# Output projection of a transformer block: four weight panels in buffers of their own, an earlier first load, the norm's running sums in PSUM

## The reference

```
y = (g_a * y_a + g_b * y_b) @ w_mix_out
x = layer_norm(ALPHA * x + mod(1, 2) * y, ln2_g, ln2_b)
h = x * (1.0 + mod(2, 1)) + mod(2, 0)
x = layer_norm(ALPHA * x + 0.5 * mod(2, 2) * swiglu(h, ffn2_w_in, ffn2_w_out), ln3_g, ln3_b)
```

## Time and profile before

| | |
|---|---|
| median of 3 runs | 1108.89 us (1108.68 to 1109.15) |
| the profiled execution | 1108.3 us, its span 1106.1 us |
| TensorE busy | 1096.5 us, 99% of the span |
| DVE / POOL / ACT busy | 527.5 / 521.6 / 412.9 us |
| granted clock | 0.999 in the mean |

### The profile page before, as it was taken

The page is one execution under the profiler, slowest core; times in us unless marked ns, Lnnn a source line. Parts: engine busy times, 40 slices in busy tenths (PEclk is TensorE's granted clock), DMA queues, the critical chain, the costliest instruction groups (busy, mean ns, idle before and its releaser), DMA issues.

```text
span 1106.1 us, 15348 instructions
## 1 busy us (share of the span) xinstructions
PE 1096.5 (99%) x5574; PEld 895.8 (81%) x5574; DVE 527.5 (48%) x924; ACT 412.9 (37%) x665; POOL 521.6 (47%) x277
## 2 busy tenths in 40 slices
PE   9999999999999999999999999999999999999997
PEld 6788888888888997875578887898888888888887
DVE  6677756441121269268747678784322223111105
ACT  4453232223222274278623233357322222232223
POOL 1044544444444464459824453646444444445452
PEclk9999999999999999999999999999999999999999
DMA  9555554322333272210145653323433332233322
GB/s 373 200 195 203 184 174 173 106 95 86 95 98 105 74 258 96 87 38 20 49 132 201 219 182 132 120 72 134 146 121 114 114 114 95 90 92 101 105 69 76
DMA packets 53460, 142.11 MB, mean 128 GB/s; under 512 B 5793, under 2 KB 13985, under 8 KB 52129
## 3 DMA queue, kind: packets, MB, share of 16 engines
q1 hardware_dynamic: 52400, 136.25, 36.8%
q10 hardware_dynamic: 1008, 5.17, 1.3%
HBM read 139.31 MB, written 2.10 MB: 128 GB/s over the span
## 4 chain that ended last, share of the span: by engine, by line
PE 95%; DVE 2%; DMA 1%; ACT 1%; issue 1%; SPq 0%; POOL 0%; ACTq 0%; DVEq 0%
PE psum L667 29%; PE psum L669 29%; PE psum L668 29%; PE psum L1055 2%; PE psum L1106 2%; PE psum L1134 2%; DMA ada_first<-in_ada 1%; PE psum L990 1%; PE psum L697 1%; DVE acc L1919 0%; PE psum L1120 0%; DVE blocked L1663 0%; PE psum L1026 0%; POOL w_lo L568 0%; PE psum L796 0%
## 5 line engine op out<-in xcount | busy, mean ns | idle before, releaser
L568 POOL TENSOR_TENSOR w_lo<-raw,w_hi 128x1024 fp32r<-128x1024 f32 x177 | 437.1, 2473 | 532.8 <-ACT w_hi L1230 532.5
L667 PE MATMUL psum<-h_hi,w_hi 128*128 128x512 f32 (+1 forms) x1008 | 381.7, 379 | 1.1 <-POOL h_lo L617 1.0
L668 PE MATMUL psum<-h_lo,w_hi 128*128 128x512 f32 (+1 forms) x1008 | 378.7, 376 | 0.0
L669 PE MATMUL psum<-h_hi,w_lo 128*128 128x512 f32 (+1 forms) x1008 | 378.6, 376 | 0.0
L1230 ACT ACTIVATE w_hi<-raw 128x1024 fp32r<-128x1024 f32 x183 | 191.7, 1052 | 153.1 <-PE psum L669 95.8
L667 PEld LDWEIGHTS psum<-h_hi,w_hi 128*128 128x128 f32 x1008 | 189.6, 188 | 41.0 <-issue 4.5
L669 PEld LDWEIGHTS psum<-h_hi,w_lo 128*128 128x128 f32 x1008 | 189.7, 188 | 34.4
L668 PEld LDWEIGHTS psum<-h_lo,w_hi 128*128 128x128 f32 x1008 | 189.7, 188 | 33.8
L1919 DVE SCALAR_TENSOR_TENSOR acc<-ada_raw,cact,acc 128x512 f32<-128x512 f32 x98 | 138.2, 1446 | 15.6 <-DMA ada_raw<-in_ada_w 15.5
L667 PE MATMUL psum<-act_hi,w_hi 128*128 128x512 f32 (+1 forms) x396 | 145.3, 367 | 0.0
L669 PE MATMUL psum<-act_hi,w_lo 128*128 128x512 f32 (+1 forms) x396 | 144.7, 365 | 0.0
(11 more groups left out here) (269 smaller groups left out, 1009.0 us busy)
## 6 DMA issues: line engine op xcount, KB each, us to landing
raw<-in_ffn_in SPq DMA_DIRECT2D x82, 512.0 KB, 3.3
ada_raw<-in_ada_w SPq DMA_DIRECT2D x112, 256.0 KB, 3.5
raw<-in_ffn_out SPq DMA_DIRECT2D x32, 448.0 KB, 3.3
raw<-in_mix_w SPq DMA_DIRECT2D x27, 512.0 KB, 3.3
ada_first<-in_ada SPq DMA_DIRECT2D x8, 1024.0 KB, 11.1
raw<-in_ffn_out SPq DMA_DIRECT2D x16, 512.0 KB, 3.5
raw<-in_branch_w SPq DMA_DIRECT2D x8, 512.0 KB, 3.8
raw<-in_mixout_w SPq DMA_DIRECT2D x8, 512.0 KB, 3.3
```

What stands on the lines that cost most here:

```text
L568: gp.tensor_tensor(w_lo[:, slot, :], raw[:, slot % 2, :], w_hi[:, slot, :].bitcast(F32), ALU.subtract).then_inc(split_done, 1)
L667: pe.matmul(o_, w_hi[:, wslot, ws], xh, start=first, stop=False)
L668: pe.matmul(o_, w_hi[:, wslot, ws], xl, start=False, stop=False)
L669: return pe.matmul(o_, w_lo[:, wslot, ws], xh, start=False, stop=last)
```

## The change

- **Own buffers.** Panels 4 to 7 of the output projection are split into `late_hi` and `late_lo`, which lie where the branches' operands lay; they wait for the branches to be through, and for no slot. The feed-forward's first four panels then wait for the panel that used their slot, eight before.
- **Order of splits on ACT.** A list, MIXOUT_SPLIT, says how many panels are split ahead of the square of tile m; panel 11 is split between the first two late squares, ahead of the first root. POOL splits the feed-forward's first four panels ahead of all low parts of h.
- **First load.** SP issues panel 0 of the projection ahead of the last six modulation pieces.
- **Fold.** The third fold stands on DVE behind mixed_lo(7), and `sum_modulation` on TensorE in panel 1, behind its third k.
- **PSUM.** The running sum lies in bank 3, the squares of tiles 1 to 4 alternate in banks 5 and 4; the last sum goes back to `scr`.

```diff
@@
 LOW_BANK = {1: 4, 2: 0}
+OWN = 4
+OWN_FROM = B_MIXOUT + KT - OWN
+SUMS_BANK, SQ_BANK = 3, 4
+MIXOUT_SPLIT = [4, 6, 8, 9, 11]
@@
         o_lo = at("o_lo", [P, 4, T], R + 81920, F32R)
         w1k = at("w1k", [P, PAIRS, 256], R + 73728)
         tokens = at("tokens", [P, TT, D], O_HHI)
+        late_hi = at("late_hi", [P, OWN, 1024], R + 57344, F32R)
+        late_lo = at("late_lo", [P, OWN, 1024], R + 73728, F32R)
         mixed_hi = at("mixed_hi", [P, KT, T], R, F32R)
         mixed_lo = at("mixed_lo", [P, KT, T], R + 16384, F32R)
         tab = at("tab", [P, 2, 2, T], R + 32768)
@@
             for i in range(3 * KT):
                 if i >= 3:
                     branch_panel(i + 2)
+                if i == 3 * KT - 3:
+                    panel(B_MIXOUT, mixout_w[0, :, :], slot=B_MIXOUT % 2)
                 for q in range(2 * (i % 3), 2 * (i % 3) + 2):
                     ada_unit("mix", i // 3, q)
-            for m in range(KT):
+            for m in range(1, KT):
                 p = B_MIXOUT + m
                 panel(p, mixout_w[m, :, :], slot=p % 2)
             feed_forward(2)
@@
                 gp.wait_ge(split_hi, p + 1)
                 gp.tensor_tensor(w_lo[:, slot, :], raw[:, slot % 2, :], w_hi[:, slot, :].bitcast(F32),
+                                 ALU.subtract).then_inc(split_done, 1)
+            def own_split(i):
+                p = OWN_FROM + i
+                gp.wait_ge(split_hi, p + 1)
+                gp.tensor_tensor(late_lo[:, i, :], raw[:, p % 2, :], late_hi[:, i, :].bitcast(F32),
                                  ALU.subtract).then_inc(split_done, 1)
             def splits(start, end):
@@
                             alibi((u + 3) // 2, ((u + 1) % 2,))
                         elif u < 7:
                             split(B_BRANCH + u - 3, (B_BRANCH + u - 3) % 4)
-                    splits(B_BRANCH + 4, end + 3)
+                    splits(B_BRANCH + 4, OWN_FROM)
+                    for i in range(OWN):
+                        own_split(i)
+                    splits(B_FFN2, B_FFN2 + GROUP)
                 for m in (1, 2, 3, 4):
                     low(L, 0, m)
-                split(end + 3, 3)
+                if L == 1:
+                    split(end + 3, 3)
                 for m in (6, 7):
                     low(L, 0, m)
                 for m in LOW_POOL[1]:
@@
         @block.tensor
         def _(pe):
-            def product(o_, wslot, kk, xh, xl, first, last):
+            def product(o_, wslot, kk, xh, xl, first, last, w=(w_hi, w_lo)):
                 ws = slice(kk * P, (kk + 1) * P)
-                pe.matmul(o_, w_hi[:, wslot, ws], xh, start=first, stop=False)
-                pe.matmul(o_, w_hi[:, wslot, ws], xl, start=False, stop=False)
-                return pe.matmul(o_, w_lo[:, wslot, ws], xh, start=False, stop=last)
+                pe.matmul(o_, w[0][:, wslot, ws], xh, start=first, stop=False)
+                pe.matmul(o_, w[0][:, wslot, ws], xl, start=False, stop=False)
+                return pe.matmul(o_, w[1][:, wslot, ws], xh, start=False, stop=last)
             def panel_over_h(p, wslot, b, h_wait=None):
@@
                 for k in range(4):
                     ins = product(bank(b + 3), p % 4, 4 + k, o_hi[:, k, :], o_lo[:, k, :], k == 0, k == 3)
                 ins.then_inc(panels_used, 1)
+            def mixout_panel(m):
+                p = B_MIXOUT + m
+                return (p - OWN_FROM, (late_hi, late_lo)) if p >= OWN_FROM else (p % 4, (w_hi, w_lo))
             pe.wait_ge(br_mixed, KT - 1)
-            sum_modulation(2, 3, 6)
             for m in range(LATE[2][0]):
+                slot, w = mixout_panel(m)
                 p = B_MIXOUT + m
                 if m >= 2:
                     pe.wait_ge(z_done, Z0[2] + m - 1)
@@
                 for k in range(KT):
                     if m == 0:
                         pe.wait_ge(br_split, k + 1)
-                    ins = product(bank(m % 2), p % 4, k, mixed_hi[:, k, :], mixed_lo[:, k, :],
-                                  k == 0, k == KT - 1)
+                    ins = product(bank(m % 2), slot, k, mixed_hi[:, k, :], mixed_lo[:, k, :],
+                                  k == 0, k == KT - 1, w)
+                    if m == 1 and k == 2:
+                        sum_modulation(2, 3, 6)
                 ins.then_inc(panels_used, 1)
             pe.wait_ge(ada_taken, 2)
             for h in range(2):
                 for i, m in enumerate(LATE[2]):
                     p = B_MIXOUT + m
+                    slot, w = mixout_panel(m)
                     if h == 0 and i < 2:
                         pe.wait_ge(z_done, Z0[2] + m - 1)
                     else:
@@
                     if h == 0:
                         pe.wait_ge(split_done, p + 1)
                     for k in range(KT):
-                        ins = product(psum[:, (m + h) % 2, part(h)], p % 4, k, mixed_hi[:, k, part(h)],
-                                      mixed_lo[:, k, part(h)], k == 0, k == KT - 1)
+                        ins = product(psum[:, (m + h) % 2, part(h)], slot, k, mixed_hi[:, k, part(h)],
+                                      mixed_lo[:, k, part(h)], k == 0, k == KT - 1, w)
                         if k == KT - 1:
                             ins.then_inc(panels_used if h else half_made, 1)
                         if h == 1:
@@
             def split(p, slot, filled):
                 act.wait_ge(raw_landed[slot % 2], 16 * filled)
-                need(act, panels_used, p - 3)
+                if isinstance(p, int) and OWN_FROM <= p < B_FFN2:
+                    act.wait_ge(panels_used, B_MIXOUT)
+                    act.activation(late_hi[:, p - OWN_FROM, :], raw[:, slot % 2, :], ACT.Copy).then_inc(split_hi, 1)
+                    return
+                if isinstance(p, int) and B_FFN2 <= p < B_FFN2 + OWN:
+                    act.wait_ge(panels_used, p - 3 - OWN)
+                else:
+                    need(act, panels_used, p - 3)
                 if isinstance(p, int) and p == P_GATE:
                     act.activation(gate_w[:, :].rearrange("p (k c) -> p k c", c=32),
                                    raw[:, slot % 2, :].rearrange("p (k c) -> p k c", c=P)[:, :, 0:32],
@@
                 act.wait_ge(z_done, Z0[L] + m + 1)
                 if m >= 2:
                     act.wait_ge(q_added, QA0[L] + max(m - 2, 1))
-                act.activation(scr[:, 2 + m % 2, :], X[:, m, :], ACT.Square).then_inc(sq_done, 1)
+                to = scr[:, 2 + m % 2, :]
+                if L == 2:
+                    to = bank(SQ_BANK + m % 2) if m else scr[:, 1, :]
+                act.activation(to, X[:, m, :], ACT.Square).then_inc(sq_done, 1)
             def first_row(k):
@@
                 for i in range(late):
                     square_half(L, i, 0)
+                    if L == 2 and i == 0:
+                        split_before(p0 + 1)
+                if L == 1:
+                    split_before(p0 - 2)
                 root(0)
                 if L == 2:
                     square_half(2, 0, 1)
@@
                 act.activation(mixed_hi[:, m, :], tab[:, m % 2, 0, :], ACT.Copy).then_inc(br_hi, 1)
             act.preload_act_table(ACT.Sqrt)
             for m in range(LATE[2][0]):
-                split_before(B_MIXOUT + m + 1)
+                split_before(B_MIXOUT + MIXOUT_SPLIT[m] - 3)
                 square(2, m)
-            split_before(B_FFN2 - 2)
             norm_halves(2)
             feed_forward(2)
             act.preload_act_table(ACT.Sqrt)
@@
                     dve.wait_ge(s_added, summed[0])
                 summed[0] += 1
                 dve.wait_ge(z_done, Z0[L] + m + 1)
-                a = X[:, 0, :] if m == 1 else scr[:, 0, :]
-                dve.tensor_tensor(scr[:, 0, :], a, X[:, m, :], ALU.add).then_inc(s_added, 1)
+                total = bank(SUMS_BANK) if L == 2 else scr[:, 0, :]
+                a = X[:, 0, :] if m == 1 else total
+                to = scr[:, 0, :] if m == LATE[L][0] - 1 else total
+                dve.tensor_tensor(to, a, X[:, m, :], ALU.add).then_inc(s_added, 1)
             def squares(L, m):
                 dve.wait_ge(sq_done, Q0[L] + m + 1)
                 if m > 1:
                     dve.wait_ge(q_added, QA0[L] + m - 1)
+                if L == 2:
+                    dve.tensor_tensor(scr[:, 1, :], bank(SQ_BANK + m % 2), scr[:, 1, :], ALU.add).then_inc(q_added, 1)
+                    return
                 a = scr[:, 2, :] if m == 1 else scr[:, 1, :]
                 dve.tensor_tensor(scr[:, 1, :], a, scr[:, 2 + m % 2, :], ALU.add).then_inc(q_added, 1)
@@
                 dve.wait_ge(x_scaled, 8 * (L - 1) + m + 1)
                 dve.wait_ge(s_added, summed[0])
                 summed[0] += 1
-                dve.tensor_tensor(scr[:, 0, :], scr[:, 0, :], X[:, m, :], ALU.add).then_inc(s_added, 1)
+                total = bank(SUMS_BANK) if L == 2 else scr[:, 0, :]
```

(5 more changed lines are left out.)

## The result

The changed kernel takes **1113.1 us** in the median of 7 runs (1112.37 to 1113.93), the kernel before, run beside it, 1108.75 us (1108.46 to 1109.15). The ratio is 1.0040, with a 95% interval from 1.0030 to 1.0049: slower, by 4.4 us. The forecast was 1109.4, with a range up to 1111.4. It was wrong: the change is slower, where I had forecast no difference that can be measured. The profiled execution took 1113.6 us, its span is 1111.4 (before 1108.3 and 1106.1), so the traces have 5.3 us to explain.

A forecast was written before the change was run, and what follows sets the result against it. TensorE, busy 1096.5 of 1106.1 us, was taken to bound the kernel. +1.35 (the new gap, with the fold's -1.14 inside) - 0.84 = +0.5 us on the median 1108.89 gave 1109.4 us, range 1106.8 to 1111.4.

The forecast's parts named there:

- Part 1: Moving the third fold and its product into panel 1: the 1.58 us gap goes, the 0.44 product stays, -1.14 us.
- The two readiness margins: In the fold's move: mixed_lo(7) ready 1.1 us before TensorE needs it, the fold 1.2 us before its product.
- Part 2: Panel 0 of the output projection loaded before six modulation loads: nothing lost, by some 2 us; needed for Part 1.
- Part 3: Own buffers, earlier splits: ACT's panel 10 split delays tile 4's square; new 2.5 us TensorE gap before third late half.
- the round: Cycle of the raw double buffer: load 3.3, ACT to POOL 1.13, POOL 2.38, issue 0.04, together 6.85 us.
- Rival 2: The new gap drops TensorE's clock to 1.2 GHz for 24 products: +2.9, in all +3.4, 1112.3 us; chance 0.10.
- Part 4: No weight splits behind the first root: DVE's held sum of squares falls from 1.26 to 0.42 us, -0.84 us.
- Sums and squares in PSUM: no cost, no gain by themselves: On DVE: at most 0.05 us more each, hidden; the 2 us blocks they end had not delayed TensorE.
- the factor column: DVE's 8-column, SBUF-only operation before tile 0's square: held by a POOL split; without a hold the sum would be -0.1.
- rival 1: No new gap before the third late half, panel 10's split coming in time: -2.0 us, 1106.9; chance 0.22.

The follow-up runs named there:

- fold_back: fix_order with the third fold and its product ahead of the output projection again; 1107.22 us, ratio to the kernel before 0.9988.
- load_back: fix_order with panel 0 of the projection loaded behind the six modulation pieces again; 1108.46 us, ratio to the kernel before 0.9998.
- fix_order: The changed kernel with ACT splitting panel 10 between the second and third late squares, panel 11 behind the third; 1106.17 us, ratio to before 0.9979.
- one_number: The changed kernel with MIXOUT_SPLIT's last entry 10, not 11: panels 10 and 11 both split between the first two late squares; 1108.16 us, ratio 0.9999.
- gap_full: The changed kernel with 18 dummy 128x128 products of ones on TensorE between the second and third late half; 1111.17 us, ratio to before 1.0022.
- gap_half: The changed kernel with 10 dummy 128x128 products of ones on TensorE between the second and third late half; 1112.51 us, ratio to before 1.0029.
- no_own: The kernel before with only the early load of panel 0 and the moved fold and product; 1107.2 us, ratio 0.9987.
- sbuf_sums: fix_order with running sums and squares in SBUF again; 1111.75 us, ratio to the kernel before 1.0030.
- splits_late: fix_order with panels 10 and 11 split behind the first root, as before; 1107.06 us, ratio to the kernel before 0.9987.
- psum_only: The kernel before with only the running sum and squares moved to PSUM; 1108.69 us, ratio 1.0003.

## Why the prediction was wrong

**Part 1 (forecast -1.14): the gap right, the number by luck: two errors cancel.** TensorE's shift at the first late half is -1.10, and undoing the fold costs 1.05. The gap was worth 1.58, but the 0.44 us between the folded product and the first output product were not the product's price: 683.20 to 710.75 is 27.55 us, against 27.34 before, so 0.21. The other 0.23 were the wait for panel 0's split, which the prediction did not see behind the fold (see fold_back); the early load took it away. An upstream shift of 0.27 took that back. The two readiness margins held.

**Part 2: the reading was right** (nothing lost, needed for part 1), and load_back shows what it keeps away: 2.3 us.

**Part 3 (forecast gap 2.5 us): the mechanism right, the size wrong. This is the first step that failed.** Everything in the chain was as described, to the line that TensorE waits for; fix_order shows it. From start to start the stop was 4.71 us. TensorE was due at 716.50, 0.05 later than forecast; the restart came 2.26 later than forecast, because the load did: split from 718.10, forecast 715.7. Two terms of the round were mis-sized, the load and the issue. Of the issue this is the row, from the timeline of SP's queue:

```profile
713.93 1.61 SPq L472 DMA_DIRECT2D raw<-in_ffn_in  x1
```

- The first load of the round, panel 4, took 1.6 us longer than forecast. It took 4.9 us (issued 691.07, split from 695.99), where the earlier trace rows gives 3.3. I had taken 3.3 from the median of all issues and asked no bound of it. With panel 8's first issue at 706.35, panel 10's came at 713.56 where my round gives 712.09, 1.5 late.
- Of panel 10's three transfers, the second took 1.61 us to issue instead of 0.43. The last so went out at 715.59, and 4.54 us passed from the first issue to landing, forecast 3.6.
- My bounds for the gap were 0.6 less and 1.5 more, for POOL's splits; a late load had no bound at all. That is why even the range's upper end fell short.

What made the load and the issue long stays open. From issue to split panel 4's load took 4.5 to 5.0 us in the change, fix_order, one_number, gap_full, gap_half, load_back and no_own, but 3.1 in fold_back and at most 3.7 in sbuf_sums and splits_late; in the kernel before it was 3.2. The long issue stood at the second or third transfer of panel 10 in the change and six of its variants, with 1.4 to 2.0 us (gap_half has the longest), at one of panel 11 in fold_back (1.16), and in sbuf_sums there was none up to 720; in the kernel before one of 1.48 us stood at 731.44, where nobody waited. So neither belongs to the changed order as such. No run varied either by itself.

**Rival 2 (the gap costs the clock, chance 0.10): it happened. This is the second step that failed, the chance.** Its price was nearly right: 2.9 for 24 products forecast, 2.5 measured. All 24 ran at the lower level, but there they stood 0.21 us apart, not 0.24. I spoke against it with 1.60 us that cost nothing, but asked only about a gap of 2.5. With a bound for the load of the size that it then had, 1.6 us, the gap would have reached 4 us, and this rival would have needed a large part of the chance. By gap_full an idle time of 2.69 us kept the clock in ten of eleven executions: the forecast's own gap would most likely not have cost it. So the two errors are one: the wrong size carried the wrong chance.

**Part 4 (forecast -0.84): right.** The shift between the turned sums of the first and second half is -0.84, and splits_late puts 0.9 us on it.

**"Sums and squares in PSUM: no cost, no gain by themselves": right for the kernel before (psum_only), wrong for the change (sbuf_sums, 5.6 us).** I read the holds in the trace of before, where two of over 2 us hit DVE while it had time, and carried that over to a schedule with six. The Trainium skill's rule, which I had cited for the factor column (held, as forecast: 1.57 us at 691.87), applied to every sum that met a split. In the sum of the prediction it changed nothing, since the change has the sums in PSUM; it was a wrong reading of what carries what.

**In the sum:** forecast -1.14 + 2.5 - 0.84 = +0.5; measured -1.10 + 4.71 + 2.53 - 0.84 = +5.3. Without the gap and the clock it would be -1.9, near rival 1's -2.0; fix_order gives that kernel, at -2.0 between the profiled executions and -2.5 between the medians.

## What to carry to other kernels

In an engine that works in written order, a wait for a load must not stand ahead of short work that another engine's chain needs: put the short work first, and the load's split where its data is sure to be there. When a forecast rests on when a load lands, take its bound from the longest of its kind in the trace, issue time included, and ask at each end of the range whether the gap it makes is long enough to cost TensorE's clock. And a measure against port conflicts is worth what the schedule around it makes of it: nothing in the old order, 5.6 us in the new.

## What the runs showed of the hardware

- **The clock after a gap.** In the traces of this kernel idle times of 1.52 and 2.69 us inside full streams left TensorE's level at 2.4 GHz; 3.46, 3.58 and 4.55 us were followed by 1.2 GHz. The same kernel can go either way: by the mean clock of the span gap_half, 3.58 us in its trace, fell in three of five executions, one_number in three of ten, gap_full in one of eleven. So a single trace without a fall does not clear a gap. In gap_half the fall came not with the gap but after the restart: 1.00 still in 720 to 722, 0.58 behind it, so the stretch behind the gap has to be read, not the gap itself. After the 4.55 us the level was back 5.5 us after the restart. The Trainium skill, TensorE: Matmul & The Clock Gate, section "Why this matters for your kernels", warns of such gaps; the traces agree, though not every execution fell.
- **A small product is cheap, and a second wait can hide in its row.** The two products of 128x96 cost 0.21 us inside panel 1, and 0.21 behind the stop in fold_back too; the 0.44 us of before held a wait for a weight split. 128x128 products of ones ran at 0.12 us each.
- **A DMA issue and a load can be slow.** One issue of 128 KB on SP's queue took 1.61 us where its neighbours took some 0.43, and one load of 512 KB took from 3.1 us (fold_back) to 5.0 (gap_full, load_back) in variants of one kernel.
